# mLSTM head norm: summing a head's two channel tiles on VectorE ahead of the float32 matmul over channels

## The reference, cut to what matters

```python
def ml_output(h, o, norm_w, w_out):
    mu = jnp.mean(h, axis=-1, keepdims=True)
    var = jnp.mean(jnp.square(h - mu), axis=-1, keepdims=True)
    hn = (h - mu) * lax.rsqrt(var + EPS) * norm_w[:, None, :]
    return (jax.nn.sigmoid(o) * hn) @ w_out
```

## Time and profile before

| | before |
|---|---|
| median of three runs | 1835.96 us |
| the runs | 1835.76, 1838.89, 1835.96 us |
| span of the profiled execution, first to last instruction | 1837.7 us |
| its own time, apart from the span | not given |
| busy: TensorE matmul, VectorE, ScalarE, GpSimd | 94%, 57%, 38%, 35% |
| chain that ended last, TensorE's share | 81% |
| mean granted TensorE clock (share of 2.4 GHz) | 0.974 |

### The profile page before, as it was taken

How to read it: one execution, slowest core, us unless ns; L and a number is a source line. 1 busy time by engine, 2 the same in 40 slices (tenths; PEclk the granted TensorE clock), 3 DMA queues, 4 the chain that set the end, 5 groups by cost and what they waited for, 6 DMA issues and landing times.

```text
span 1837.7 us, 29895 instructions
## 1 busy us (share of the span) xinstructions
PE 1731.0 (94%) x11444; PEld 1618.9 (88%) x11444; DVE 1053.5 (57%) x1651; ACT 694.9 (38%) x1074; POOL 642.0 (35%) x292
## 2 busy tenths in 40 slices
PE   6899999788999999999978999998889999999996
PEld 3688888678988999899977999997879999999996
DVE  1277767655875614767337545544668781387823
ACT  3255555534433212322235445644263331133323
POOL 3212221235533333323534232122555333233444
PEclk8999999889999999999999999999999999999998
DMA  9722122111355223453211112110212222222221
GB/s 379 261 70 69 52 69 68 32 35 58 132 188 196 75 75 115 157 198 123 83 62 41 41 53 66 45 52 29 69 46 76 73 86 75 69 69 80 82 79 57
DMA packets 54034, 169.35 MB, mean 92 GB/s; under 512 B 7728, under 2 KB 13232, under 8 KB 53936
## 3 DMA queue, kind: packets, MB, share of 16 engines
q1 hardware_dynamic: 47600, 163.79, 25.8%
q10 hardware_dynamic: 6336, 4.20, 0.7%
HBM read 159.04 MB, written 4.72 MB: 89 GB/s over the span
## 4 chain that ended last, share of the span: by engine, by line
PE 81%; DVE 7%; ACT 4%; DVEq 2%; issue 2%; DMA 2%; POOL 1%; SPq 1%; ACTq 0%; POOLq 0%
PE pj L602 69%; DMA awr<-in_w_ada 2%; PE mO L1001 2%; PE psO L779 2%; PE pfrow L627 1%; PE psS L744 1%; DVE pr L1862 1%; PE psT L760 1%; ACT pr L1264 1%; POOL X L550 1%; DVE sm L1847 1%; PE mS L957 1%; DVE h32t L1883 1%; PE mT L1026 1%; PE mT L1018 0%
## 5 line engine op out<-in xcount | busy, mean ns | idle before, releaser
L473 POOL TENSOR_TENSOR wlo<-wraw,whi 128x1024 fp32r<-128x1024 f32 (+1 forms) x130 | 333.0, 2562 | 825.2 <-ACT whi L1138 825.2
L602 PE MATMUL pj<-Hh,whi 128*128 128x320 f32 x2400 | 570.3, 319 | 35.7 <-issue 13.7
L602 PE MATMUL pj<-Hh,wlo 128*128 128x320 f32 x2400 | 553.5, 312 | 0.0
L602 PE MATMUL pj<-Hl,whi 128*128 128x320 f32 x2400 | 548.5, 312 | 2.2 <-POOL Hl L503 1.2
L602 PEld LDWEIGHTS pj<-Hh,whi 128*128 128x128 f32 x2400 | 403.8, 191 | 65.9 <-issue 51.7
L602 PEld LDWEIGHTS pj<-Hl,whi 128*128 128x128 f32 x2400 | 405.4, 190 | 3.7 <-POOL Hl L496 1.8
L602 PEld LDWEIGHTS pj<-Hh,wlo 128*128 128x128 f32 x2400 | 407.9, 191 | 0.0
L1138 ACT CAST whi<-wraw 128x1024 fp32r<-128x1024 f32 (+1 forms) x180 | 199.5, 1109 | 313.4 <-PE pj L602 278.4
L1762 DVE SCALAR_TENSOR_TENSOR fcv<-fus,vec,fcv 128x127 f32<-128x127 f32 (+1 forms) x176 | 231.7, 1357 | 15.6 <-issue 15.6
L1717 DVE SCALAR_TENSOR_TENSOR X<-pj,mods,X 128x128 f32<-128x128 f32 (+1 forms) x144 | 54.5, 434 | 266.9 <-PE pj L602 266.6
L602 PE MATMUL pj<-Gl,whi 128*128 128x320 f32 x704 | 160.4, 309 | 0.0
(11 more groups left out here) (308 smaller groups left out, 2051.3 us busy)
## 6 DMA issues: line engine op xcount, KB each, us to landing
wraw<-in_w_up SPq DMA_DIRECT2D x88, 512.0 KB, 3.3
fwr<-in_w_ada SPq DMA_DIRECT2D x56, 512.0 KB, 5.8
wraw<-in_w_dn SPq DMA_DIRECT2D x32, 704.0 KB, 4.1
awr<-in_w_ada SPq DMA_DIRECT2D x40, 512.0 KB, 10.6
wraw<-in_w_qkv SPq DMA_DIRECT2D x24, 512.0 KB, 3.4
wraw<-in_w_mlin SPq DMA_DIRECT2D x24, 512.0 KB, 3.2
sx<-h32t SPq DMA_DIRECT2D x128, 32.0 KB, 2.0
wraw<-in_w_wo SPq DMA_DIRECT2D x8, 512.0 KB, 3.3
```

Of the source, the lines that this page charges most:

```text
L473: nc.gpsimd.tensor_tensor(wlo[k][:, 0:width], wraw[k][:, 0:width], whi[k][:, 0:width].bitcast(F32), ALU.subtract).then_inc(w_lo, 1)
L602: last = mm(out[:, c, 0:HALF], w, x[:, j, c * HALF:(c + 1) * HALF], start=(j == 0 and n == 0), stop=(j == n_k - 1 and n == 2))
```

## The change

VectorE adds `hO[:, 0, :]` and `hO[:, 1, :]` into `ss` (`m_tile_sum`), so that the mean takes one matmul for a half instead of two; after ScalarE has squared, VectorE adds the two tiles of squares (`m_square_add`), and the square sum also takes one. The mean now waits for the first addition (`mh_sum`) and the square sum for the second (`msq_sum`). The first stands on VectorE ahead of `m_combine(h, 1)`, the second behind `m_v_lo(h, 1)`. For the last head both are in line with `m_centre`.

```diff
@@ TensorE
             def m_mean(h):
-                pe.wait_ge(mo_free, 3 * h + 3)
+                pe.wait_ge(mh_sum, h + 1)
                 m_wait(("c", h))
                 for c in range(2):
-                    for w in range(2):
-                        last = mm(mT[:, c, 0:HALF], ones[:, :], hO[:, w, c * HALF:(c + 1) * HALF], start=(w == 0), stop=(w == 1))
+                    last = mm(mT[:, c, 0:HALF], ones[:, :], ss[:, c * HALF:(c + 1) * HALF], start=True, stop=True)
                 last.then_inc(mt_full, 1)
 
             def m_square_sum(h):
-                pe.wait_ge(msq_ready, h + 1)
+                pe.wait_ge(msq_sum, h + 1)
                 m_wait(("s", h))
                 for c in range(2):
-                    for w, sq in enumerate((ss[:, c * HALF:(c + 1) * HALF], rs[:, c, :])):
-                        last = mm(mT[:, c, 0:HALF], ones[:, :], sq, start=(w == 0), stop=(w == 1))
+                    last = mm(mT[:, c, 0:HALF], ones[:, :], ss[:, c * HALF:(c + 1) * HALF], start=True, stop=True)
                 last.then_inc(mt_full, 1)
@@ VectorE
+            def m_tile_sum(h):
+
+                dve.wait_ge(mo_free, 3 * h + 3)
+                tt(ss[:, :], hO[:, 0, :], hO[:, 1, :], ALU.add).then_inc(mh_sum, 1)
+
+            def m_square_add(h):
+
+                dve.wait_ge(msq_ready, h + 1)
+                tt(ss[:, :], ss[:, :], rs[:, :, :].rearrange("p a b -> p (a b)"), ALU.add).then_inc(msq_sum, 1)
+
@@ m_head(h), heads 1 to 3
                     m_turned(h, 0)
+                    m_tile_sum(h - 1)
                     m_combine(h, 1)
                     m_v_lo(h, 0)
                     m_centre(h - 1)
                     m_v_lo(h, 1)
+                    m_square_add(h - 1)
@@ behind the last head
             m_turned(ML_HEADS - 1, 4)
+            m_tile_sum(ML_HEADS - 1)
             m_centre(ML_HEADS - 1)
+            m_square_add(ML_HEADS - 1)
             m_final(ML_HEADS - 1)
```

More of the change, by code:

```diff
@@ L343, in hybrid_step @@
                 "ml_split", "mc_hi", "c0_in", "c0_split", "mv_full", "mv_hi", "mv_lo", "c_out", "mout_done", "sig_ready"))
+        mh_sum, msq_sum = sem("mh_sum"), sem("msq_sum")
         block = ctx.enter_context(nc.Block())
```

## The result

The change costs time. Four runs of each kernel gave 1848.67 us (1845.21 to 1849.85) against 1837.43 (1835.76 to 1839.58), a ratio of 1.0052 with a 95% interval of 1.0034 to 1.0070. In a later series twelve runs of the changed kernel gave 1844.57 us (1840.55 to 1849.30) against 1838.24 (29 runs, 1832.39 to 1840.77), a ratio of 1.0036 [1.0024, 1.0049]. So it is about 6.3 us slower, and single runs of one kernel lie up to 9 us apart. The first median lies above the predicted range (1833.5 to 1844.5), the second 0.1 us above it.

What follows compares the result with a forecast made beforehand. It took TensorE as bound at first reading, but VectorE-to-ScalarE handovers with about 0.6 us slack as deciding. Heads +2.6, +2.6, +0.85 and tail -0.65 gave +5.4 on 1835.96: 1841.4 us, 8-in-10 range 1833.5 to 1844.5.

Steps and rivals of the forecast that it cites:

- The tail: Last head's norm: halved mean and square sum outweigh the additions, GpSimd being idle there; -0.65 us.
- Rival 1: TensorE stays the bound and VectorE's additions lie in its idle time: -8.6 us at most, chance 0.17.
- the sum of the squares: Heads 1 to 3: addition slowed by GpSimd's split ends at 1103.24; square sum follows, +0.26 behind it, VectorE +2.29.
- The collision: Heads 1 and 2: GpSimd's split gets between VectorE's two m_final products; second product ends at about 1116.0.
- the +2.6 of head 1: Head 1's forecast lengthening, through late m_final products, the next combine and ScalarE's copy of tile o0; +2.6 us.
- rival 2: Heads 1 and 2: m_final's second product starts ahead of GpSimd's split; +0.9 in all, 1836.9 us, chance 0.22.
- rival 3: TensorE's clock falls in the new stalls, about 1.3 to 2 us each; +8 to +10 in all, chance 0.11.
- Head 3: Products get through before the split; only ScalarE's late copy of o1 delays the head, +0.85 us.

Runs made afterwards that it cites:

- e3: Kernel before, with mean and square sum taking only one channel tile (one matmul a half) and no additions: 1834.60 us, ratio 0.9975 to the kernel before.
- e6: Changed kernel with TensorE's square sum two places later, behind other TensorE work: 1843.75 us, ratio 1.0033 to the kernel before.
- e10: Changed kernel plus five unread small float32 matmuls on TensorE ahead of the square sum's wait in heads 1 to 3: 1841.37 us, ratio 1.0017 to the kernel before.
- e5: Changed kernel with GpSimd's weight split made to wait for the second addition in heads 1 to 3: 1843.14 us, ratio 1.0030 to the kernel before.
- e4: Changed kernel with both additions kept but unread, mean and squares keeping two matmuls a half: 1850.26 us, ratio 1.0065 to the kernel before.
- e7: Changed kernel with the second addition moved behind the low part of the turned weights on VectorE: 1837.31 us, ratio 0.9989 to the kernel before.
- e2: Changed kernel with the first addition left out and the mean as before, only the squares changed: 1839.76 us, ratio 1.0008 to the kernel before.

## Why the prediction was wrong where it was wrong

**What held** is the sign and the first half of the mechanism. The additions lengthen a chain from VectorE's combine over ScalarE to the copy that TensorE waits for. The first addition was put at 0.74 and took it from ScalarE's idle time exactly. TensorE's stall behind it was 1.04 us. The second addition was put at 1.63 us beside GpSimd's split and took 1.62. The tail was put at -0.65 and measured -0.65. Rival 1 (-8.6 us) is out: even with no additions at all e3 gives -4.7.

**The step that failed first** is in the sum of the squares: "TensorE starts the square sum at 1103.3 where it was 1101.97", that is, right behind the addition. On the same footing (2.18 us taken off) it started at 1104.25, 0.95 later. The missing term is the low part behind the addition, 0.94 us. The list of uses of `mT` makes the square sum wait for it, and before it was met to within 0.15 us. I took 0.11 us of "issue" in the chain for no wait at all. So head 1's share was +1.2 at this place instead of +0.26.

**The second error followed from it.** The forecast had VectorE's products at 1112.2 and the split at 1112.5 to 1112.7. On the same footing they came at 1112.20 and 1113.32. VectorE's side was right to 0.01 us; the split was late because ScalarE's copy now waited for a TensorE that was itself 0.95 late. The collision missed, and with it the +2.6 of head 1 (rival 2, put at 0.22). That the collision was otherwise priced rightly is shown by e6, where the square sum doesn't hold TensorE up: +5.25 against +5.4.

**The third is the clock,** rival 3 at 0.11. It was priced rightly (1.3 to 2 us a fall, measured 1.56) and had too small a chance, since the new stalls in the heads were read as at most 1.4 us where one is 2.1. It also counted any fall as one more, while head 3 has as many as before. e10 takes the falls behind the square sums away, and heads 1 and 2 come down to +1.2 each, which is +0.26 and the missing 0.95. So the changed kernel is rivals 2 and 3 together with a longer stall, and its +5.92 in the profile lies near the forecast's +5.4 by accident. Head 3 shows it: put at +0.85, it measures +2.61.

**The absolute number** also had a low base: 1835.96 came from three runs, and longer series of the kernel before gave 1838.2 to 1839.3. With the trace's +5.9 on 1838.24 one comes to 1844.2, and 1844.57 was measured. The first four runs, 11.2 us above the kernel before, are not explained beyond that; their profiled execution shows 5.9 in the mLSTM and 2.2 in a part that the change doesn't touch.

## What to carry to other kernels

An instruction put into an engine's queue delayed what stood behind it there, by 0.74 us (mean) and 1.62 us (squares). So list who waits for those later instructions, the reuse of PSUM tiles included: here the one that mattered was met to within 0.15 us and showed only as 0.11 us of "issue". Work that is to come off the bounding engine should go to an engine that idles at that moment and holds nothing up behind it: here GpSimd, at 1.57 us an addition, gained where VectorE at 0.82 lost. And where a change adds two stalls close together, price the clock with them.

## What was not expected of the hardware

- GpSimd gets in between two VectorE products that stand back to back in the queue. In e6 the split was asked for 0.29 us into the first, and 3.78 us went by for the pair instead of 1.56. In e5 and e6 the waiting engine won over the next instruction of the one at work, as in the earlier trace rows.
- The clock fell behind stalls of 1.04 and 2.10 us (changed kernel, heads 2 and 3) and behind 2.09 (e4, head 2), but not in head 1 of either or at the square sum in head 3 of e4, and not behind 1.04 and 1.20 to 1.30 us (e5, e7) or 1.69 alone (e2). Yet in head 3 of the kernel before it fell behind a single stall of 1.88 us, and behind the same stall of the changed kernel (ended at 1260.53) it did not. What tells these places apart was not found.
- Filling a stall with matmuls that nobody reads made the kernel faster (e10 against the changed kernel, 3.2 us).
